# Moving the centre tap of a depthwise convolution from VectorE to ScalarE in a gated FFN

## The reference

```python
def conv_ffn(x, w_in, b_in, conv_w, conv_b, w_out, b_out):
    h = x @ w_in + b_in
    hp = jnp.pad(h, ((0, 0), (1, 1), (0, 0)))
    h = hp[:, :-2] * conv_w[0] + hp[:, 1:-1] * conv_w[1] + hp[:, 2:] * conv_w[2] + conv_b
    u, g = jnp.split(h, 2, axis=-1)
    return (u * jax.nn.gelu(g, approximate=False)) @ w_out + b_out
```

## Time and profile before

| what | value |
|---|---|
| median of 3 runs | 3079.19 us (3075.08 to 3079.32) |
| profiled execution, its own time | 3077.33 us |
| its span | 3075.3 us |
| mean granted TensorE clock | 0.964 |
| busy over the span: PE, DVE, POOL, ACT | 92%, 59%, 40%, 29% |

### The profile page before, as it was taken

How to read it: one execution, slowest core, us unless ns; L and a number is a source line. 1 busy time by engine, 2 the same in 40 slices (tenths; PEclk the granted TensorE clock), 3 DMA queues, 4 the chain that set the end, 5 groups by cost and what they waited for, 6 DMA issues and landing times. The chain is left out here.

```text
span 3075.3 us, 37768 instructions
## 1 busy us (share of the span) xinstructions
PE 2817.0 (92%) x13323; PEld 2317.3 (75%) x13323; DVE 1809.7 (59%) x2182; ACT 901.5 (29%) x1306; POOL 1225.8 (40%) x845
## 2 busy tenths in 40 slices
PE   7999999869899999999978888887698999999998
PEld 6788887758778788888857777776477778888886
DVE  3666666645565555555745666666466655555557
ACT  3455444532211111111224444444322111111111
POOL 2444444234643323333544444443256332333335
PEclk9999999979999999999989999998699999999999
DMA  3000002214211111111221111110232111111111
GB/s 112 27 28 27 27 27 65 58 50 151 63 48 48 48 41 43 54 46 48 69 67 32 40 39 41 44 34 19 96 110 71 48 48 41 41 55 48 48 48 69
DMA packets 212626, 162.85 MB, mean 53 GB/s; under 512 B 34939, under 2 KB 194251, under 8 KB 212555
## 3 DMA queue, kind: packets, MB, share of 16 engines
q1 hardware_dynamic: 212411, 161.38, 17.8%
q10 hardware_dynamic: 144, 0.52, 0.0%
HBM read 137.24 MB, written 24.64 MB: 53 GB/s over the span
## 5 line engine op out<-in xcount | busy, mean ns | idle before, releaser
L1129 PE MATMUL ff_ph<-XTh,WH 128*128 128x512 f32 x1408 | 549.7, 390 | 6.8 <-PEq L41 6.8
L1129 PE MATMUL ff_ph<-XTl,WH 128*128 128x512 f32 x1408 | 549.0, 390 | 0.0
L1129 PE MATMUL ff_ph<-XTh,WL 128*128 128x512 f32 x1408 | 548.9, 390 | 0.0
L1067 POOL TENSOR_SCALAR WH<-raw_weights 128x1024 fp32r<-128x1024 f32 x128 | 153.0, 1195 | 844.9 <-PE ff_ph L1129 472.3
L1277 DVE TENSOR_SCALAR ff_C<-ff_H,ff_par 128x1024 f32<-128x1024 f32 x88 | 199.1, 2262 | 429.1 <-ACT ff_H L1225 428.4
L1069 POOL TENSOR_TENSOR WL<-raw_weights,WH 128x1024 fp32r<-128x1024 f32 x128 | 340.0, 2656 | 10.7
L1129 PEld LDWEIGHTS ff_ph<-XTh,WH 128*128 128x128 f32 x1408 | 265.1, 188 | 62.7 <-issue 7.6
L1129 PEld LDWEIGHTS ff_ph<-XTh,WL 128*128 128x128 f32 x1408 | 265.0, 188 | 55.2
L1129 PEld LDWEIGHTS ff_ph<-XTl,WH 128*128 128x128 f32 x1408 | 265.1, 188 | 54.9
L1225 ACT ACTIVATE ff_H<-ff_ph,ff_par 128x1024 f32<-128x1024 f32 x88 | 98.2, 1116 | 571.3 <-PE ff_ph L1129 571.3
L1270 DVE TENSOR_TENSOR X<-ff_po,X 128x512 f32<-128x512 f32 x288 | 191.8, 686 | 102.5 <-PE ff_po L1143 102.5
(11 more groups left out here) (215 smaller groups left out, 5927.3 us busy)
## 6 DMA issues: line engine op xcount, KB each, us to landing
raw_weights<-in_ffn_w_in SPq DMA_DIRECT2D x88, 512.0 KB, 3.8
raw_weights<-in_ffn_w_out SPq DMA_DIRECT2D x44, 512.0 KB, 3.5
raw_weights<-in_attn_w_qkv SPq DMA_DIRECT2D x24, 512.0 KB
raw_weights<-in_na_w_qkv SPq DMA_DIRECT2D x24, 512.0 KB, 4.7
wo_oraw<-heads_t SPq DMA_DIRECT2D x16, 512.0 KB, 4.5
rpb_rows<-da_rows SPq DMA_DIRECT2D x2, 3840.0 KB, 26.5
na_B<-rpb_rows SPq DMA_DIRECT2D x32, 224.0 KB, 3.9
da_E<-in_x SPq DMA_DIRECT2D x8, 512.0 KB, 6.0
```

The source lines that it names most:

```text
L1067: nc.gpsimd.tensor_scalar(wh[:, slot], wraw[:, raw_slot], 1.0, 1.0, ALU.mult, ALU.mult).then_inc(w_high, 1)
L1129: last = nc.tensor.matmul(out[:, at], wt[:, slot, k * P:(k + 1) * P], x[:, k, at], start=(k == 0 and n == 0), stop=(k == KT - 1 and n == 2))
```

## The change

In the FFN stages `take` makes two passes over the up tile in PSUM. The first writes H as before. The second writes the centre tap straight to C: scale is the tap w1, bias is b_in * w1 + conv_b, which VectorE works out once per stage in a small tile `centre` (128x44, two instructions). The semaphore `up_out`, for which VectorE and PE wait, is raised behind the second pass. For parity 0 the second pass waits for `a_low`, since the pair before still needs C until its low part is made; VectorE waited for that at the same place in its own order already. L1277 is gone from `conv`.

```diff
+        centre = m.sb("centre", [P, 2, NT])
+        centre_step = m.sem("centre_step")
...
-
-            def take(a, parity, idx, first=False):
+            act.wait_ge(centre_step, 2)
+
+            def take(f, parity, idx, first=False):
+                a = 2 * f + parity
                 act.wait_ge(up_done, a + 1)
                 if not first:
                     act.wait_ge(conv_done, a - 1)
                 nc.scalar.activation(H[:, parity, 1:S + 1], ph[parity][:].rearrange("p k n -> p (k n)"), ACT.Identity,
-                                     bias=par[:, 0, bass.ds(idx, 1)]).then_inc(up_out, 1)
+                                     bias=par[:, 0, bass.ds(idx, 1)])
+                if parity == 0 and not first:
+                    act.wait_ge(a_low, f)
+                nc.scalar.activation(C[:, parity], ph[parity][:].rearrange("p k n -> p (k n)"), ACT.Identity,
+                                     bias=centre[:, 1, bass.ds(idx, 1)],
+                                     scale=par[:, 2, bass.ds(idx, 1)]).then_inc(up_out, 1)
...
-                take(2 * f, 0, f, first)
-                take(2 * f + 1, 1, f + FT, first)
+                take(f, 0, f, first)
+                take(f, 1, f + FT, first)
                 gate(f)
...
             dve.wait_ge(par_set, 1)
+            nc.vector.tensor_tensor(out=centre[:, 0], in0=par[:, 0], in1=par[:, 2], op=ALU.mult).then_inc(centre_step, 1)
+            dve.wait_ge(centre_step, 1)
+            nc.vector.tensor_tensor(out=centre[:, 1], in0=centre[:, 0], in1=par[:, 4], op=ALU.add).then_inc(centre_step, 1)
...
                 dve.wait_ge(up_out, a + 1)
-                nc.vector.tensor_scalar(c, h[:, 1:S + 1], tap[2], tap[4], ALU.mult, ALU.add).then_inc(conv_link, 1)
-                dve.wait_ge(conv_link, 2 * a + 1)
                 nc.vector.scalar_tensor_tensor(out=c, in0=h[:, 0:S], scalar=tap[1], in1=c, op0=ALU.mult,
                                                op1=ALU.add).then_inc(conv_link, 1)
                 if between is not None:
                     add(between, 0)
-                dve.wait_ge(conv_link, 2 * a + 2)
+                dve.wait_ge(conv_link, a + 1)
```

## The result

| | before | after |
|---|---|---|
| median of 5 runs | 3079.19 us (3075.08 to 3083.87) | 3056.18 us (3050.71 to 3062.80) |
| profiled execution, span | 3075.3 us | 3052.4 us |
| mean granted TensorE clock | 0.964 | 0.966 |
| busy, DVE / ACT | 1809.7 / 901.5 us | 1651.9 / 998.4 us |

The ratio is 0.993, with a 95% interval from 0.991 to 0.9951. The forecast, 3060 with a range from 3052 to 3068, is a ratio of 0.9938 and lies inside.

What follows compares the result with a forecast made beforehand. PE was taken to bound the FFN, with waits for VectorE's adds behind GpSimd's hold. Two stages of 8 x 0.89 + 2.02 + 0.50 gave 19.3 us, hence a median of 3060 us, range 3052 to 3068.

Steps and rivals of the forecast that it cites:

- What bounds: FFN stages: PE's own pace, plus waits for VectorE's adds in nine rounds a stage and one wait at each end.
- The two waits: PE at outputs 4 and 5 of a round, for add 0 and add 1: 1.18 and 0.30 us.
- L1279 is held as L1277 was: Round's second tile: L1279, now first, is held by GpSimd's L1069 and ends 1.08 us after it; unheld 1.28.
- all waits go: Rival: L1279 isn't held, both adds come ahead of PE; 34 us gained in all, 3045 us; chance 0.05.
- a fixed price of a hold: Rival: held L1279 costs some 3.3 us from its own start, no steady-round gain; 3076 us; chance 0.07.
- The second pass: ScalarE's added pass from PSUM: up_out comes 1.15 us behind the first pass, hidden behind GpSimd's hold up to 2.3.
- ScalarE becomes the bound: Rival: up_out comes too late behind a second pass longer than 3.07 us; at 3.5, 3084 us; chance 0.03.
- Steady rounds: Eight rounds a stage: L1279 ends at 2600.34 instead of 2601.23, gaining 0.89 us each, 7.1 us a stage.
- First round: First round of each FFN stage: output 5 starts at 2400.55 instead of 2402.57, gain 2.02 us.
- the backlog: VectorE's lateness from the first pairs, held by GpSimd's bias adds; four L1277 of up to 2.9 us leave it.
- The end: End of each FFN stage: L1069 takes 2.39 instead of 2.89, so PE's wait of 0.6 shrinks by 0.50 us.
- Edits at nothing: The two `centre` instructions, their wait, the stage's first second pass and the a_low wait were put at no cost.

Runs made afterwards that it cites:

- run 5: Changed kernel, but ScalarE makes the centre tap only for parity 1, VectorE for parity 0 as before; 3060.37 us, ratio 0.9936.
- run 6: Changed kernel, but ScalarE makes the centre tap only for parity 0, VectorE for parity 1; 3076.10 us, ratio 0.9995.
- run 1: Kernel before, with GpSimd's split at the round's second tile held until output 7 of the down projection is done; 3040.36 us, ratio 0.9876.
- run 2: Changed kernel, with GpSimd's split at the round's second tile held until output 7 of the down projection is done; 3044.60 us, ratio 0.9881.
- run 8: Changed kernel, with add 0 ahead of the convolution and add 1 between the outer taps in a round's second tile; 3044.86 us, ratio 0.9881.
- run 3: Changed kernel, with a third ScalarE pass copying the up tile to an unread spare tile between the two others; 3060.81 us, ratio 0.9942.
- run 4: Changed kernel, with both GpSimd's split held until output 7 is done and a third ScalarE pass into a spare tile; 3059.75 us, ratio 0.9926.
- run 7: Kernel before, with add 0 ahead of the convolution and add 1 between the outer taps in a round's second tile; 3050.86 us, ratio 0.9905.

## Why the prediction was right, point by point

**What bounds.** Right, and shown by runs 5 and 6: the one place in a round that counts is the second tile. The two waits were sized a little low. The slow start of a first matmul was put at 0.11 us, but the prediction's own rows give 1.50 - 1.36 = 0.14; with that the place costs 1.76 a round and not 1.70, which is what runs 1, 2 and 8 gain.

**L1279 is held as L1277 was.** Right, and the step on which all hung. The end was put at 1.08 us after GpSimd's; it is 1.09 in the changed kernel, 1.08 in run 3. Without the hold (run 2) it takes 1.29. The rival that all waits go falls, and so does that of a fixed price of a hold: with starts 0.91 apart in the round, the left tap took 2.42 and 1.50 and ended at the same distance from GpSimd. The Trainium skill, SBUF — State Buffer, section "SBUF: two separate sides", on the shared port pair, says whichever of the two starts first has the pair for its whole instruction and the other fully blocks. These traces agree: of the 1.28 us that the left tap takes alone, 1.08 to 1.09 come after GpSimd's end, in the round of the changed kernel and in run 3. The other way round, GpSimd's subtraction takes 2.89 instead of 2.39 where L1277 had started 0.17 ahead of it.

**The second pass.** Estimated at 1.15 behind the first, measured 2580.74 - 2579.65 = 1.09; it takes 1.19 itself and overlaps by 0.10. Nothing depended on it, as run 3 shows with 0.91 us more. The prediction's limit of 2.3 us for what the hold hides is 2.2 by its own numbers (2600.34 - 1.28 - 0.18 - 2596.70 = 2.18); run 3 went to 2.0, and the limit itself was not tried. Its price for a place where GpSimd is idle was too high too: it gave 0.3 us, but from the start of ScalarE's first pass to that of the left tap it is 2.36 in run 2 and 2.26 in run 1, so 0.1. The rival in which ScalarE becomes the bound was real as a mechanism, but not at this length: run 4 shows it at work, with a third pass and without GpSimd's hold.

**Steady rounds.** 0.89 forecast; measured 0.91 in the rounds shown, 0.90 by the medians of all eight.

**First round.** 2.02 forecast. Counted from the turned parameters, output 5 started at 2402.57 - 2338.4 = 64.17 us before and starts at 2387.33 - 2325.2 = 62.13 after: 2.04. Here is the round's start in the changed kernel:

```profile
2373.61 2.91 DVE L1289 SCALAR_TENSOR_TENSOR ff_C<-ff_H,ff_par,ff_C 128x1024 f32<-128x1024 f32 x1 [1.55 <-ACT ff_C L1233]
2376.68 1.28 DVE L1294 SCALAR_TENSOR_TENSOR ff_C<-ff_H,ff_par,ff_C 128x1024 f32<-128x1024 f32 x1 [0.16 <-DVE ff_C L1289]
2382.53 2.35 DVE L1289 SCALAR_TENSOR_TENSOR ff_C<-ff_H,ff_par,ff_C 128x1024 f32<-128x1024 f32 x1 [4.57 <-ACT ff_C L1233]
```

VectorE is done with the tile before at 2377.96 and idle for 4.57 us: the backlog is gone. Not all four of the removed L1277 were needed for that: run 5 kept the two for parity 0, and its output 5 starts at 2386.63 - 2324.5 = 62.13 us as well.

**The end.** 0.50 forecast. PE's step from the early to the late half of the last down projection was 1.01 us in the old trace (a wait of 0.6); it is 0.52 now:

```profile
3007.47 0.39 PE L1155 MATMUL ff_ph<-WH,WL 128*128 128x512 f32 x1
3007.99 0.47 PE L1155 MATMUL ff_po<-WH 128*128 128x512 f32 x1
```

**The sum.** 19.3 forecast, 19.4 found inside the FFN stages. That the median is 3056 and not 3060 comes from outside them, as far as the traces can tell: 3.5 us of the difference between the two spans are there, and the prediction had nothing for it. That the median fell by 23 us and not by 19 is therefore not to the forecast's credit.

**Edits at nothing.** The new wait for a_low cost nothing on the path, though VectorE is idle behind it for 1.55 us in the first round, here as in run 6.

## What to carry to other kernels

When an instruction on the path takes far longer than elsewhere, look for who holds its engine before moving it: what comes next in the queue inherits the hold, and here the place had 1.76 us a round to give, of which the change got back 0.91. Starting the neighbour later, when it is idle for 19.9 us anyway, gave the whole 1.76 without moving any work off VectorE. Queuing the adds ahead of the held instruction gave 1.36 in the kernel before and, together with the change, 1.76. A cost that is hidden should be named with what hides it, since the next edit may remove that.

## What the runs showed of the hardware that was not expected

An add with one operand in PSUM is not held. In run 1 one starts 1.32 us into GpSimd's subtraction, and both take their usual time:

```profile
2520.21 0.69 DVE L1272 TENSOR_TENSOR X<-ff_po,X 128x512 f32<-128x512 f32 x1 [0.67 <-PE ff_po L1145]
```

```profile
2518.89 2.42 POOL L1069 TENSOR_TENSOR WL<-raw_weights,WH 128x1024 fp32r<-128x1024 f32 x1
```

In run 7 add 0 runs from 2579.82 in 0.69 us while GpSimd's subtraction starts at 2579.87 and takes its usual 2.39; the centre tap right behind is held:

```profile
2579.87 2.39 POOL L1069 TENSOR_TENSOR WL<-raw_weights,WH 128x1024 fp32r<-128x1024 f32 x1
```

The neighbourhood stage doesn't repeat itself. The granted clock between 1560 and 2220 us, the same code in all kernels, differs between executions while it is 1.00 in the FFN rounds (2400 to 2900 us in the same three traces). The columns are: window, length, PE, PEld, DVE, ACT, POOL busy with counts, clock, DMA share, GB/s. First comes the kernel after, then run 3, then run 2:

```profile
1560.00:2220.00 660.00, 561.32 (x2811) 451.10 (x2810) 380.90 (x702) 295.71 (x548) 264.21 (x238) 0.93 0.17 43
```

```profile
1560.00:2220.00 660.00, 558.69 (x2828) 449.11 (x2827) 381.04 (x702) 297.33 (x550) 264.92 (x239) 0.95 0.17 44
```

```profile
1560.00:2220.00 660.00, 566.61 (x2778) 454.54 (x2778) 378.05 (x701) 293.99 (x546) 261.39 (x235) 0.90 0.16 42
```

The stretch between the FFN marks took 838.6, 837.2 and 848.0 us in these three. The five runs of the changed kernel go the same way, the longer the lower the clock: spans of 3048.6, 3052.4, 3054.1, 3059.3 and 3060.7 us at mean clocks of 0.968, 0.966, 0.965, 0.961 and 0.961. From the shortest to the longest that is 12 us, more than half of what the change gains. What makes the clock differ was not tried. For a change of this size the length of the rounds in a trace says more than the medians: in the changed kernel the eight distances are all 66.13 to 66.15 us.
